# The MLP of a one-core decoder step: inner tiles of both halves in turns, their high parts at once, weight blocks from the seventh up tick, shared sums added in the last up stage

## What is computed

```python
def merge_and_mlp(h, gates, y_a, y_b, y_c, w_out, norm_mlp_g, w_up, w_down):
    mixed = gates[0] * y_a + gates[1] * y_b + gates[2] * y_c
    h = h + mixed @ w_out
    hn = rmsnorm(h, norm_mlp_g)
    return h + jnp.square(jax.nn.relu(hn @ w_up)) @ w_down
```

## Time and profile before

| what | value |
|---|---|
| median of 3 runs | 1050.03 us (1047.0 to 1050.32) |
| the profiled execution | 1050.15 us |
| its span in the profile | 1048.4 us |
| TensorE, matmuls busy | 1007.7 us (96%) |
| VectorE busy | 631.7 us (60%) |
| ScalarE busy | 432.7 us (41%) |
| GpSimd busy | 306.7 us (29%) |
| mean TensorE clock granted, whole span | 0.992 |

### The profile page before, as it was taken

The page is one execution under the profiler, slowest core; times in us unless marked ns, Lnnn a source line. Parts: engine busy times, 40 slices in busy tenths (PEclk is TensorE's granted clock), DMA queues, the critical chain, the costliest instruction groups (busy, mean ns, idle before and its releaser), DMA issues.

```text
span 1048.4 us, 21764 instructions
## 1 busy us (share of the span) xinstructions
PE 1007.7 (96%) x8426; PEld 918.2 (88%) x8426; DVE 631.7 (60%) x1042; ACT 432.7 (41%) x828; POOL 306.7 (29%) x150
## 2 busy tenths in 40 slices
PE   7999999999999999999999999989998998989996
PEld 6987877886878777899999999989997998989996
DVE  6215478789255554255444665779668947984634
ACT  6114557576243322252333334454245425423432
POOL 1323132222222120111121112343433634343720
PEclk9999999999999999999999999999999999999998
DMA  8588886775976477524223245445845767459102
GB/s 297 188 286 299 297 290 226 264 262 182 320 252 194 154 256 239 194 84 164 96 86 101 81 140 233 166 156 202 298 175 205 281 216 257 155 191 359 63 2 82
DMA packets 65673, 209.50 MB, mean 200 GB/s; under 512 B 7833, under 2 KB 10138, under 8 KB 63266
## 3 DMA queue, kind: packets, MB, share of 16 engines
q1 hardware_dynamic: 65282, 207.75, 56.5%
q10 hardware_dynamic: 288, 0.35, 0.1%
HBM read 200.59 MB, written 51.48 MB: 240 GB/s over the span
## 4 chain that ended last, share of the span: by engine, by line
PE 76%; DVE 12%; issue 6%; ACT 4%; DMA 1%; SPq 1%; DVEq 0%; ACTq 0%
PE G L1611 52%; PE Z L1611 10%; PE S L1611 10%; PE OU L1611 2%; PE TR L1614 2%; DVE tn L1166 1%; DVE slow L1166 1%; DVE hT L1166 1%; DVE bsum L1166 1%; DVE mt L1169 1%; ACT whi L846 1%; DVE tl L1166 1%; DVE hidl L1166 1%; ACT hidh L846 1%; ACT msq L1083 1%
## 5 line engine op out<-in xcount | busy, mean ns | idle before, releaser
L1611 PE MATMUL G<-xh,whi 128*128 128x260 f32 x1288 | 373.9, 290 | 14.0 <-DVE xl L1169 7.3
L1611 PE MATMUL G<-xl,whi 128*128 128x260 f32 x1288 | 364.7, 283 | 0.0
L1611 PE MATMUL G<-xh,wlo 128*128 128x260 f32 x1288 | 364.2, 283 | 0.0
L1611 PEld LDWEIGHTS G<-xh,whi 128*128 128x128 f32 x1288 | 243.2, 189 | 58.5 <-issue 50.4
L812 POOL TENSOR_TENSOR wlo<-wraw,whi 128x1024 fp32r<-128x1024 f32 x60 | 147.3, 2456 | 492.4 <-ACT whi L846 492.4
L1611 PEld LDWEIGHTS G<-xl,whi 128*128 128x128 f32 x1288 | 243.4, 189 | 0.0
L1611 PEld LDWEIGHTS G<-xh,wlo 128*128 128x128 f32 x1288 | 243.3, 189 | 0.0
L846 ACT ACTIVATE whi<-wraw 128x1024 fp32r<-128x1024 f32 (+1 forms) x84 | 88.0, 1048 | 226.5 <-PE G L1611 214.0
L812 POOL TENSOR_TENSOR wlo<-mraw,whi 128x1024 fp32r<-128x1024 f32 x31 | 76.9, 2485 | 116.1 <-ACT whi L846 116.1
L1166 DVE TENSOR_TENSOR hidl<-msq,hidh 128x260 fp32r<-128x260 f32 x52 | 65.9, 1270 | 44.6 <-ACT hidh L846 44.6
L822 POOL TENSOR_TENSOR mlow<-mraw,bhigh 128x512 fp32r<-128x512 f32 x36 | 58.6, 1645 | 86.8 <-DVE bsum L1166 66.7
(11 more groups left out here) (325 smaller groups left out, 2261.7 us busy)
## 6 DMA issues: line engine op xcount, KB each, us to landing
wraw<-in_w_in_dram SPq DMA_DIRECT2D x65, 512.0 KB, 5.7
kv<-in_kpool_dram SPq DMA_DIRECT2D x128, 256.0 KB, 3.8
kv<-in_vpool_dram SPq DMA_DIRECT2D x128, 256.0 KB, 3.5
mraw<-in_w_up_dram SPq DMA_DIRECT2D x32, 512.0 KB, 5.4
out_win_k_kept_dram<-in_cache_win_k_dram SPq DMA_DIRECT2D x8, 2047.0 KB, 11.5
out_win_v_kept_dram<-in_cache_win_v_dram SPq DMA_DIRECT2D x8, 2047.0 KB, 9.8
mraw<-in_w_down_dram SPq DMA_DIRECT2D x30, 512.0 KB, 3.4
wraw<-in_w_ab_dram SPq DMA_DIRECT2D x8, 512.0 KB, 3.3
```

The costliest lines, as they stand in the source:

```text
L1611: return nc.tensor.matmul(out, lhsT, rhs, start=start, stop=stop, **kw)
```

## The change

Five edits, all in the MLP.

1. The order of inner tiles in stages 0 to 2 becomes 0, 4, 1, 5, 2, 6, 3, 7 (`ORDER`, `place_of`): the up unit in turn t loads that tile's column of `w_up`, and the products find it through `TURN_OF`.
2. ScalarE makes the highs of a tick right after its own square, and VectorE the sums T1 to T4 of a tick in the same tick (`hid_sums`); the lows stay a tick behind (`hid_lows`). For a tile with T2 to T4 the order of names is now B, T2, T3, T4.
3. The first pair's blocks move: sums after up ticks 6 and 8 (before 7 and 9), the seven highs after ticks 6 to 12, one each (before 7, 8, 8, 10, 10, 11, 12), VectorE's lows after 8 to 11 (before 10 to 13), GpSimd's after 9, 11 and 13 (before 10, 11 and 12).
4. On GpSimd the split of a whole weight unit comes before a plain block's low of the same tick.
5. The twelve additions of `eacc` leave the product ticks of stage 2. They are made one at a time in the first twelve up ticks of stage 3 (`add_shared`), without waiting for each other, and the down ticks wait for them.

```diff
+ORDER = (0, 4, 1, 5, 2, 6, 3, 7)
+def place_of(t):
+    return ORDER[t % KC] if t // KC < SEVEN else t % KC
...
-            unit("up", KC * q + t, "w_up", KC * q + t, KC, [("up", 0, KC, "x", KC * q + t)])
+            unit("up", KC * q + t, "w_up", KC * q + place_of(KC * q + t), KC, [("up", 0, KC, "x", KC * q + t)])
...
     if g % (KC // 2):
-        return [at("prod", g - 1, j) for j in range(7)]
-    last = at("up", 2 * g + KC - 1)
-    return [last - 8 + j for j in range(7)]
+        t = [at("prod", g - 1, j) for j in range(7)]
+        return [t[j] for j in (0, 0, 2, 2)], [t[j] for j in (0, 1, 1, 3, 3, 4, 5)], t[3:7], t[3:6]
+    t = [at("up", 2 * g + KC - 1) - 15 + j for j in range(16)]
+    return [t[j] for j in (6, 6, 8, 8)], [t[j] for j in (6, 7, 8, 9, 10, 11, 12)], t[8:12], [t[j] for j in (9, 11, 13)]
...
-        _names = ("T2", "T3", "B", "T4")
+        _names = ("B", "T2", "T3", "T4")
...
-                for g, i in PLAIN_LOWS_AFTER.get(k, []):
-                    plain_low(g, i)
                 for v in SPLIT_AFTER.get(k, []):
                     if not LO[v][0]:
                         split_lo(v)
+                for g, i in PLAIN_LOWS_AFTER.get(k, []):
+                    plain_low(g, i)
...
                 nc.scalar.activation(full("B", t, h), mt[:, h], ACT.Square).then_inc(m_sq, 1)
-                if n % (2 * KC):
-                    hid_high(n - 1)
-                if n % (2 * KC) == 2 * KC - 1:
-                    hid_high(n)
-
-            def hid_high(n):
-                t, h = n // 2, n % 2
                 act.wait_ge(m_sq, n + 1)
                 for name in SPLITS[n]:
...
-                if q == SEVEN - 1 and j == 6:
-                    dve.wait_ge(dve_took, k + 1)
-                    for part in (hT[:, t, half(1)], hT[:, t + 1, half(0)], hT[:, t + 1, half(1)]):
-                        link(tt(part, part, eacc[:, t // 2], ALU.add))
+            def add_shared(n):
+                p, part = n // 3, n % 3
+                dve.wait_ge(dve_took, at("prod", NPAIRS - KC // 2 + p, 6) + 1)
+                dst = hT[:, 2 * p + (part > 0), half((1, 0, 1)[part])]
+                tt(dst, dst, eacc[:, p], ALU.add).then_inc(shared_made, 1)
...
                     if n % (2 * KC):
-                        hid_split(n - 1)
+                        hid_lows(n - 1)
+                    hid_sums(n)
+                    if tile // KC == SEVEN and n % (2 * KC) < 3 * KC // 2:
+                        add_shared(n % (2 * KC))
                     if n % (2 * KC) == 2 * KC - 1:
-                        hid_split(n)
+                        hid_lows(n)
...
                     dve.wait_ge(dve_took, at("prod", (tile - KC) // 2, 6) + 1)
+                    dve.wait_ge(shared_made, 3 * KC // 2)
...
-                    t = t0 + c0_ + kc
+                    t = TURN_OF[t0 + c0_ + kc]
```

More of the change, by code:

```diff
@@ L130, in pair_ticks @@
     if g % (KC // 2):
-        return [at("prod", g - 1, j) for j in range(7)]
-    last = at("up", 2 * g + KC - 1)
-    return [last - 8 + j for j in range(7)]
+        t = [at("prod", g - 1, j) for j in range(7)]
+        return [t[j] for j in (0, 0, 2, 2)], [t[j] for j in (0, 1, 1, 3, 3, 4, 5)], t[3:7], t[3:6]
+    t = [at("up", 2 * g + KC - 1) - 15 + j for j in range(16)]
+    return [t[j] for j in (6, 6, 8, 8)], [t[j] for j in (6, 7, 8, 9, 10, 11, 12)], t[8:12], [t[j] for j in (9, 11, 13)]
 SUMS_AFTER, LOWS_AFTER, HIGHS_AFTER, PLAIN_LOWS_AFTER = {}, {}, {}, {}
 for _g in range(NPAIRS):
[L138 to L146, removed]
+    for _after, _ticks in zip((SUMS_AFTER, HIGHS_AFTER, LOWS_AFTER, PLAIN_LOWS_AFTER), pair_ticks(_g)):
+        for _i, _t in enumerate(_ticks):
+            _after.setdefault(_t, []).append((_g, _i))
+TURN_OF = {t // KC * KC + place_of(t): t for t in range(DFF // P)}
 SPLITS, HID_N, SUM_N, HID_AFTER, SUM_AFTER = [], {}, {}, [], []
 for _n in range(2 * DFF // P):
-    _t, _c, _h = _n // 2, _n // 2 % KC, _n % 2
+    _t, _c, _h = _n // 2, place_of(_n // 2), _n % 2
     if _t // KC >= SEVEN or _h == 0:
@@ L567, in decoder_step @@
         m_sq, t_made, hid_hi, hid_lo = (sem(n) for n in ("m_sq", "t_made", "hid_hi", "hid_lo"))
+        shared_made = sem("shared_made")
         s_made, b_hi, b_lo_dve, b_lo_pool = (sem(n) for n in ("s_made", "b_hi", "b_lo_dve", "b_lo_pool"))
@@ L618, in split_of @@
         def split_of(name, t, h):
-            c = t % KC
+            c = place_of(t)
             if name == "B" or name == "T1":
@@ L1372, in take, with hid_sums @@
                     dve.wait_ge(dve_took, at("prod", (tile - KC) // 2, 6) + 1)
+                    dve.wait_ge(shared_made, 3 * KC // 2)
                     dve.wait_ge(made, k + 1)
                     tt(hT[:, t, half(h)], hT[:, t, half(h)], src, ALU.add).then_inc(dve_took, 1)
-            def hid_split(n):
-                t, h = n // 2, n % 2
-                dve.wait_ge(m_sq, n + 1)
+            def hid_sums(n):
+                t = n // 2
                 for name in SPLITS[n]:
@@ L1381, in hid_split @@
                         continue
-                    c = t % KC - (0 if name == "T1" else KC // 2)
+                    dve.wait_ge(m_sq, n + 1)
+                    c = place_of(t) - (0 if name == "T1" else KC // 2)
                     if name == "T1":
@@ L1392, in hid_split, with hid_lows @@
                     tt(full(name, t, 1), a, b, ALU.subtract).then_inc(t_made, 1)
+            def hid_lows(n):
+                t, h = n // 2, n % 2
                 for name in SPLITS[n]:
```

## The result

| what | before | changed |
|---|---|---|
| median, four runs each | 1049.99 us (1047.0 to 1050.32) | 1031.67 us (1030.87 to 1031.85) |
| ratio, 95% interval | | 0.983 [0.9812, 0.9849] |
| profiled execution; its span | 1050.15; 1048.4 us | 1031.57; 1029.8 us |
| mean TensorE clock granted | 0.992 | 0.997 |

What follows compares the result with a forecast made beforehand. TensorE's own work bounds the kernel; only its standstills and slow-clock stretches can be regained. Of 20.7 + 4.5 = 25.2 us, 7.8 stay, so 17.4 us off 1050.15 gives 1032.8 us, range 1029.0 to 1041.0.

Steps and rivals of the forecast that it cites:

- Standstills before, 20.7 us, and clock, 4.5 us: TensorE in the MLP before the change: 20.7 us standing still, 4.5 us lost to three stretches at the lower clock.
- The shared adds (edit 5): Stage 2's long `eacc` wait of 3.89 us and six short bank waits go; twelve adds in stage 3 cost nothing.
- The last up unit: Unit 7's `wlo` wait in stages 0 to 2: 0.8 us left in stages 1 and 2; stage 0 1.8, unit 6 0.5.
- the chain of the prediction: Ahead of unit 7's `whi`, ScalarE no longer waits for T2 to T4: five fewer VectorE instructions, 1.7 us.
- The 0.4 us of the `mlow` ahead of the `wlo` (edit 4): On GpSimd before unit 7: an `mlow` delaying `wlo`, counted as 0.4 us in the wait before and the wait left.
- The product with T2: Stages 0 to 2: `mt` of tick 15 is 2.4 us late, leaving 1.0 us of wait for `tl` per stage.
- the T1 tile: Products of stages 0 to 2: the last T1 tile, now turn 6, brings a new wait of 0.3 us.
- Loads at nothing: Sum after up tick 6 needs its second block a tick sooner; in time by 1.4 us, so priced at nothing.
- The clock: TensorE in the MLP: all 4.5 us come back if remaining waits are at most 1.8 us; short waits might keep part.
- The rival with one fall per stage: TensorE's clock still falls once in each of stages 0 to 2: about 4.5 us more, 1037.3 us; chance 0.20.
- lateness only moves: Unit 7's `whi` stays as late, three waits of about 2.0 us remain and the clock falls: 1039.9 us; chance 0.10.
- late blocks: Second block lands after tick 6, delaying unit 7 up to 7.4 us per stage: 1054.8 us; chance 0.06, full or part.

Runs made afterwards that it cites:

- e1: Changed kernel with the twelve shared additions of `eacc` put back into stage 2's products: 1039.89 us, ratio 0.9906 to the kernel before.
- e8: Changed kernel with the twelve shared additions of `eacc` left out altogether, so part of the sum is missing: 1031.43 us, ratio 0.9824 to the kernel before.
- e3: Changed kernel with highs and sums made a tick late again, names ordered T2, T3, B, T4: 1034.2 us, ratio 0.9858 to the kernel before.
- e7: Kernel before with only the shared additions moved to stage 3's up ticks: 1043.68 us, ratio 0.9935 to the kernel before.
- e2: Changed kernel with the inner tiles in the old order 0 to 7: 1036.54 us, ratio 0.988 to the kernel before.
- e9: Changed kernel with the old tile order and the late highs and sums both restored: 1040.38 us, ratio 0.9906 to the kernel before.
- e11: Changed kernel with the old block ticks and GpSimd's old order both restored: 1033.59 us, ratio 0.984 to the kernel before.
- e5: Changed kernel with GpSimd's old order, a plain block's low ahead of a whole unit's low: 1028.81 us, ratio 0.9796 to the kernel before.
- e6: Changed kernel with GpSimd's old order and VectorE's last first-pair low after up tick 12, not 11: 1028.69 us, ratio 0.9804 to the kernel before.
- e10: Kernel before with only the new block ticks and the shared additions moved to stage 3: 1037.09 us, ratio 0.9871 to the kernel before.
- e4: Changed kernel with the first pair's blocks at their old ticks: 1033.01 us, ratio 0.9846 to the kernel before.

## Why the prediction was right

The forecast was 1032.8 us, the result 1031.67; the MLP gave 17.8 us where the sum had 17.4. Step by step:

- **Standstills before, 20.7 us, and clock, 4.5 us.** By the count over all gaps the first is 21.9 (small ones of 0.15 to 0.44 us, that of stage 3 among them, were left out), and three falls at 1.45 are 4.4. Right.
- **The shared adds (edit 5), 5.9 us, priced at nothing in stage 3.** e1 brought back 5.5 us of standstills, e8 shows nothing paid in stage 3. Right. The step named VectorE's slack as the cover. It didn't see that an add is one more instruction that GpSimd can hold: without edit 2 the last one is held, and the first down tick waits 2.4 us (e3, e7).
- **The last up unit, 0.8 us left in stages 1 and 2, 1.8 and 0.5 in stage 0.** Found from start to start 0.9, 0.9, 1.6 and 0.6. The sizes came out and **the reason does not carry them**. The step said that "ScalarE now waits for no T2 to T4" ahead of this `whi`, 1.7 us. With the old order (e2) and with the old order and the late highs (e9) such a tile stands ahead of it again, and unit 7 waits 0.60 and 0.59 us. How late `whi` starts, counted from two ticks before the end of up tick 13, tells it (that is the end of tick 11, but for e11, where unit 6 waits in between and tick 11 ends 0.5 us earlier): 5.0 us before; 3.1 in the changed kernel (786.00 less 782.9); 2.9 in e9 (788.04 less 785.1); 3.5 in e11 (788.65 less 785.1). Edits 1 and 2 alone take 1.5 of the five microseconds (e11), edits 3 and 4 alone 2.1 (e9), and all four together 1.9. So the chain of the prediction is real (it said 1.7), but it doesn't add to what edits 3 and 4 do, and is not needed beside them. I had one chain that fitted and didn't ask whether another edit alone would do as much. Nor was `whi` brought down to the 2.5 us late of the sum. The 0.8 came out near because the 0.6 us missing there and the next item's 0.4 us too many offset each other, which is luck. In stage 0 the 1.8 was half of an added-up load, a guess: the reason given, heavy tiles in the first half, is not what makes unit 7 wait longer there, since with the old order it still costs 1.4 (e2) and 1.6 us (e9).
- **The 0.4 us of the `mlow` ahead of the `wlo` (edit 4).** The sum kept the 0.4 us, though in the changed kernel no `mlow` is left ahead of that `wlo` (it starts at 787.12, `whi` ends at 787.04), and the prediction gave edit 4 no term of its own: it went into the up units' with edits 1 to 3. Edit 4 costs 2.7 us (e5). The step looked at GpSimd's own queue and left out which VectorE instruction the moved `mlow` would meet, though it had taken 0.76 us for just such a meeting.
- **The product with T2, 1.0 us, and the T1 tile, 0.3 us.** Found 0.95, 0.94, 1.18 and 0.24, 0.27, 0.28. The sizes were right again, as the net of more than the step named: edit 1 takes 1.8 us off it (e2 against the changed kernel), and edit 4 puts about 0.9 us on (gone in e5, which undoes it alone).
- **Loads at nothing.** The two sums after tick 6 run one right behind the other in each stage; no `bsum` waits for a load. Right.
- **The clock.** No fall, 4.4 us back. Right, and the caution that short waits could keep a part of the loss did not come out: nothing was lost behind the waits of 0.4 to 1.5 us. The section of the Trainium skill that the prediction names (TensorE: Matmul & The Clock Gate, "HAM oscillation — how this bites in real kernels") tells of waits for DMA that are longer than the bursts of matmuls between them; to short waits the prediction carried it over by itself. The rival with one fall per stage had its condition named (waits of more than 1.8 us) and that was not met.

The rivals "lateness only moves" and "late blocks" did not occur; e9, which undoes two edits, comes out at the first one's time (1039.9 against 1040.4), but by `tl` and `hidl` waits with falls and not by `whi`.

## What to carry to other kernels

When several edits are costed together and one chain explains the sum, ask of each edit whether the others would do as well without it: here one of five made the kernel 2.7 us slower inside a gain of 18, and its effect was on an engine that it did not touch. Where VectorE's two-input operations and GpSimd's run side by side, look at who starts while the other runs, and put GpSimd's instruction where VectorE waits for something else. And close the books: own work plus standstills plus clock falls should give the same constant for every variant; then a difference of some tenths can be read in a program whose unchanged part varies by more.

## What the runs showed of the hardware

Over the fourteen profiles the MLP has 48 waits of TensorE with brackets of 0.7 to 1.66 us and 25 of 1.82 to 3.91 us (the wait ahead of the final norm is not counted). Behind none of the 48 did the clock fall; behind 15 of the 25 it did, down to 0.51 to 0.64 in a window of 3.5 us, for 1.45 us on average. In the upper group length doesn't decide it: 1.82 us fell in e6 and not in e5, 1.94 fell and 1.97 did not (e9), 2.98 did not (before) and 2.45 did (e7). What does was not settled. Nor does a fall need a wait: those near 400 us in e1, e7, e9 and e10 came in a stretch (385 to 410 us) where TensorE has no bracket at all, only short rows of matmuls that start 0.4 to 0.5 us apart in place of 0.12, and the other ten profiles have the same rows there without a fall.

Falls also differ between executions of one kernel. The profiled one of e7, with all four of its waits fallen, took 1045.39 us at a mean clock of 0.989; two others took 1042.49 and 1042.67 at 0.993. The slowest executions of e4 (1034.4 us) and e8 (1033.48), kernels whose profiles have no fall in the MLP, have the lowest clock of their kernel as well, 0.995 where the others have 0.996 to 0.998. So falls are likely a part of the spread of 2.8 and 3.2 us, though only one execution of each can be looked into.

A fall isn't always paid. Behind unit 7's wait it shortens the next wait for VectorE by what it costs (2.17 us to 0.52, e7), since there TensorE only runs up to a bound that VectorE sets; behind unit 6's in e6 it is paid in part. Behind a wait with none to follow in its stage (e1, and e11, where the products don't wait) it is paid in full.
